# Another order for the last recurrent steps of a hybrid trunk: u split ahead of the scan, later loads, low weight halves on GpSimd

## The reference, cut to what matters

```python
proj = x @ w_in;  u, gate = split(proj)                       # 2048 x 1024 each
u = conv_b + sum(u_pad[:, tap:tap + S] * conv_w[tap] for tap in range(4))
r = sigmoid(ub @ w_a + b_a);  i = sigmoid(ub @ w_i + b_i)     # four blocks of 256 features
log_a = -8 * r * softplus(-lam);  a = exp(log_a)
bterm = sqrt(-expm1(2 * log_a)) * (i * u)
h[s] = a[s] * h[s - 1] + bterm[s]                             # along the 2048 positions
y = h * silu(gate)
out = layer_norm(alpha * x + y @ w_out)                       # "second merge"
```

## Time and profile before

| | us |
|---|---|
| three runs of the kernel before | 2414.43, 2416.19, 2415.93 |
| their median | 2415.93 |
| span of the profiled execution, first to last instruction | 2414.6 |
| TensorE busy in it | 2365.7 (98%) |
| VectorE, ScalarE, GpSimd busy | 1354.1, 1121.3, 617.7 |

### The profile page before, as it was taken

One profiled execution on the slowest core, in us unless ns is written; L12 is line 12 of the kernel. 1 busy time (PEld: TensorE's weight loads), 2 busy tenths in 40 slices (PEclk: granted clock), 3 DMA queues, 4 the chain that ended last, 5 costly groups with the idle time before them and its releaser, 6 DMA issues. The chain is left out here.

```text
span 2414.6 us, 36438 instructions
## 1 busy us (share of the span) xinstructions
PE 2365.7 (98%) x13373; PEld 2031.6 (84%) x13373; DVE 1354.1 (56%) x2772; ACT 1121.3 (46%) x2060; POOL 617.7 (26%) x718
## 2 busy tenths in 40 slices
PE   9999999999999999999999999999999999999998
PEld 7888889998888888888888888878888888887787
DVE  4221211331106888888888888836535565767733
ACT  2111111311116888888888888812014565657300
POOL 0000000000001555545555545516420000000343
PEclk9999999999999999999999999999999999999999
DMA  6443443332234455555445665275533354538762
GB/s 211 139 121 112 116 128 108 118 124 83 84 110 103 110 117 125 136 137 117 112 112 124 137 136 117 78 246 183 187 106 119 119 159 131 148 124 256 243 232 78
DMA packets 221258, 328.77 MB, mean 136 GB/s; under 512 B 17421, under 2 KB 144717, under 8 KB 215261
## 3 DMA queue, kind: packets, MB, share of 16 engines
q1 hardware_dynamic: 220568, 325.91, 47.7%
q0 software_dynamic: 512, 0.53, 0.1%
HBM read 199.89 MB, written 126.48 MB: 135 GB/s over the span
## 5 line engine op out<-in xcount | busy, mean ns | idle before, releaser
L985 DVE TENSOR_TENSOR at_pl<-at_tps,at_ph 128x512 fp32r<-128x512 f32 (+3 forms) x640 | 371.0, 604 | 15.9 <-ACT at_ph L908 15.9
L908 ACT ACTIVATE at_ph<-at_tps 128x512 fp32r<-128x512 f32 (+3 forms) x640 | 318.6, 537 | 125.4 <-PE at_tps L822 117.4
L822 PE MATMUL at_tps<-ident,at_probs 128*128 128x128 f32 x2176 | 340.4, 274 | 8.4 <-DVE at_pl L985 7.1
L380 ACT ACTIVATE pa_stg<-pa_ps 128x512 fp32r<-128x512 f32 (+1 forms) x120 | 71.7, 598 | 575.4 <-PE pa_ps L272 569.5
L842 PE MATMUL at_ops<-at_ph,at_val 128*128 128x256 f32 (+1 forms) x1152 | 315.4, 296 | 0.2 <-DVE at_pl L985 0.2
L898 ACT ACTIVATE at_probs<-at_probs,at_least 128x128 f32<-128x128 f32 (+15 forms) x256 | 308.1, 1204 | 0.0
L272 PE MATMUL pa_ps<-pa_xh,pa_wh 128*128 128x512 f32 x760 | 298.9, 393 | 0.0
L272 PE MATMUL pa_ps<-pa_xh,pa_wl 128*128 128x512 f32 x760 | 297.3, 391 | 0.0
L272 PE MATMUL pa_ps<-pa_xl,pa_wh 128*128 128x512 f32 x760 | 296.9, 391 | 0.0
L842 PE MATMUL at_ops<-at_pl,at_val 128*128 128x256 f32 (+1 forms) x1152 | 295.0, 282 | 0.0
L808 PE MATMUL at_sps<-at_k,at_q 128*128 128x512 f32 (+3 forms) x640 | 277.7, 434 | 9.7 <-DVE at_probs L977 7.2
(11 more groups left out here) (203 smaller groups left out, 4516.0 us busy)
## 6 DMA issues: line engine op xcount, KB each, us to landing
at_q<-q_halves SPq DMA_DIRECT2D x45, 512.0 KB
at_k<-k_halves SPq DMA_DIRECT2D x45, 512.0 KB
q_halves<-pa_stg SPq DMA_DIRECT2D x32, 512.0 KB, 3.8
k_halves<-pa_stg SPq DMA_DIRECT2D x32, 512.0 KB, 3.7
v_halves<-pa_stg SPq DMA_DIRECT2D x32, 512.0 KB, 3.0
y_gated<-re_work SPq DMA_DIRECT2D x32, 512.0 KB, 2.9
at_val<-v_halves SPq DMA_DIRECT2D x15, 1024.0 KB, 17.4
pa_wst<-in_attn_w_in SPq DMA_DIRECT2D x14, 1024.0 KB, 7.2
```

What stands on the lines that cost most here:

```text
L380: nc.scalar.activation(out, source(kind, s), func, scale=scale).then_inc(evac_h, 1)
L822: mm = nc.tensor.transpose(tps[c % TB][:, k, :], probs[s % ROWS][:, t0:t0 + P], ident[:, :])
L908: nc.scalar.activation(ph[g % 2][:, j * PB:j * PB + n, i % 2 * P:(i % 2 + 1) * P], tps[c % TB][:, 0:n, :], ACT.Copy).then_inc(high_out, 1)
L985: nc.vector.tensor_tensor(pl[g % 2][at], tps[c % TB][:, 0:n, :], raw(ph[g % 2][at]), ALU.subtract)\
```

## The change

VectorE's program: in step 13 `split_u(14)` moves ahead of `scan(12)`, and the steps 14 and 15 are written out in a new order, with the additions of merge tiles 0 to 3 between the parts of the recurrence; `weights_low(1, c)` is gone from it. GpSimd now makes those eight low halves. ScalarE makes the high halves of blocks 0 to 3 at the end of step 13 and those of 4 to 7 inside `nonlinear(13)`. TensorE does merge tile 1 ahead of `gate_products(15)`. SyncE's order of the last four steps is written out anew: the weights go ahead of `store_y(n-1)`, `load_u(15)` too, `load_y(1, 0)` (now four DMAs: 6 of the 8 feature blocks, then the 2 of step 12) and `load_y(1, 1)` come behind both tile stores of step 14 and ahead of `store_y(13)`, the gain and shift come ahead of `store_y(14)`.

```diff
@@ SyncE, load_y(r, j), r == 1 @@
-                    sp.wait_ge(y_stored, 32 * (STEPS - NC + j // 2 + 1))
                     if j < 4:
                         sp.wait_ge(products, chunk_done(2 + j // 2))
                     else:
                         sp.wait_ge(m_products, ST + 2 * (j - 4) + 2)
+                    if j == 0:
+                        for l in range(2):
+                            sp.dma_start(raw(m_rows(1, 0)[:, l, 0:KC - CT, :]), m_y[1][:, l, 0:KC - CT, 0:YW])\
+                                .then_inc(y_loaded[0], 16)
+                        sp.wait_ge(y_stored, 32 * (STEPS - NC + 1))
+                        for l in range(2):
+                            sp.dma_start(raw(m_rows(1, 0)[:, l, KC - CT:KC, :]), m_y[1][:, l, KC - CT:KC, 0:YW])\
+                                .then_inc(y_loaded[0], 16)
+                        return
+                    sp.wait_ge(y_stored, 32 * (STEPS - NC + j // 2 + 1))
@@ SyncE, the steps @@
-            for n in range(STEPS):
+            for n in range(STEPS - 4):
...
+            for n in range(STEPS - 4, STEPS):
+                first, second = step_tiles(n)[0]
+                if n < STEPS - 2:
+                    load_u(n + 1)
+                store_tile(first)
+                if n < STEPS - 1:
+                    load_gate(n - 1)
+                store_tile(second)
+                if n == STEPS - 2:
+                    load_y(1, 0)
+                    load_y(1, 1)
+                if n == STEPS - 1:
+                    for m in range(RING):
+                        load_residual(1, m)
+                    load_gate(n - 1)
+                    load_y(1, 2)
+                    sp.wait_ge(gates, STEPS)
+                    load_gain(1)
+                if n == STEPS - 4 or n == STEPS - 3:
+                    load_weights(n - STEPS + 4)
+                if n == STEPS - 3:
+                    load_u(n + 2)
+                    sp.wait_ge(y_stored, 32 * (STEPS - NC))
+                store_y(n - 1)
             load_gate(STEPS - 1)
-            for j in range(2, 4):
-                load_y(1, j)
-            sp.wait_ge(gates, STEPS)
-            load_gain(1)
+            load_y(1, 3)
@@ GpSimd, behind the memsets of u @@
+            for c in range(KC):
+                pool.wait_ge(m_high, KC + c + 1)
+                nc.gpsimd.tensor_tensor(m_block(1, xl, c), m_block(1, xl_raw, c), raw(m_block(1, xh, c)), ALU.subtract)\
+                    .then_inc(m_split, 1)
@@ TensorE, step 15 (merge_tile's wait counts 3 more DMAs of chunk 0) @@
                 if n == STEPS - 1:
                     merge_tile(1, 0)
+                    merge_tile(1, 1)
                 gate_products(n)
@@ ScalarE, nonlinear(13); the loop over the steps; the end @@
-                    for c in range(CP * 2):
+                    for c in range(CP * 2, KC):
                         weights_high(1, c)
...
-                if n == STEPS - 2:
-                    for c in range(CP * 2, KC):
+                if n == STEPS - 3:
+                    for c in range(CP * 2):
                         weights_high(1, c)
-            deviation(1, 0)
+            for n in range(2):
+                deviation(1, n)
             nonlinear(STEPS - 1)
@@ VectorE @@
-            for n in range(STEPS):
-                if n == STEPS - 1:
-                    for c in range(CP * 2, KC):
-                        weights_low(1, c)
+            for n in range(STEPS - 2):
                 split_u(n)
...
+                convolve(n + 1)
+                if n == STEPS - 3:
+                    split_u(n + 1)
                 if n:
                     scan(n - 1)
...
+            feed(STEPS - 3)
+            remainder(STEPS - 3)
+            convolve(STEPS - 1)
+            split_u(STEPS - 1)
+            scan(STEPS - 3)
             add_rows(1, 0)
-            norm_rows(1, 0)
+            feed(STEPS - 2)
+            add_rows(1, 1)
+            remainder(STEPS - 2)
+            scan(STEPS - 2)
+            for n in range(2):
+                norm_rows(1, n)
+            add_rows(1, 2)
             feed(STEPS - 1)
             remainder(STEPS - 1)
-            add_rows(1, 1)
+            add_rows(1, 3)
             scan(STEPS - 1)
-            norm_rows(1, 1)
-            for n in range(2, ST - 1):
+            norm_rows(1, 2)
+            norm_rows(1, 3)
+            for n in range(4, ST - 1):
```

More of the change, by code:

```diff
@@ L1434, in _ @@
             load_strip(3)
-            for n in range(STEPS):
+            for n in range(STEPS - 4):
                 before, behind = step_tiles(n)
-                tiles = (*before, *behind)
                 new_block = (n + 1) % NC == 0
-                if n + 1 < STEPS and not new_block:
+                if not new_block:
                     load_u(n + 1)
-                if n == STEPS - 2:
-                    load_y(1, 0)
-                for k, t in enumerate(tiles):
+                for k, t in enumerate((*before, *behind)):
                     store_tile(t)
                     if k == 0:
-                        if n + 1 < STEPS and new_block:
+                        if new_block:
                             load_u(n + 1)
@@ L1449, in _ @@
                             load_gate(n - 1)
-                        if n + 4 < STRIPS and not new_block:
+                        if not new_block:
                             load_strip(n + 4)
-                        if n + 4 < STRIPS and new_block:
+                        else:
                             if n + 5 < STRIPS:
@@ L1456, in _ @@
                                 load_strip(n + 4)
-                    if n and k == min(2, len(tiles) - 1):
-                        if n == STEPS - 2:
-                            load_y(1, 1)
-                        if n == STEPS - 1:
-                            for m in range(RING):
-                                load_residual(1, m)
+                    if n and k == 2:
                         store_y(n - 1)
-                        if n == STEPS - 4 or n == STEPS - 3:
-                            load_weights(n - STEPS + 4)
-                if n + 4 < STRIPS and new_block:
+                if new_block:
                     if n + 5 < STRIPS:
@@ L1525, in merge_tile @@
                 j = n // 2
-                pe.wait_ge(y_loaded[j % 4], 16 * (j // 4 + (1 if r or j % 4 >= 2 else 0) + (r * (1 if j % 4 < 2 else 2))))
+                pe.wait_ge(y_loaded[j % 4], 16 * (j // 4 + (1 if r or j % 4 >= 2 else 0) + (r * (1 if j % 4 < 2 else 2))
+                                                  + (3 if r and j % 4 == 0 else 0)))
                 if r == 0:
@@ L1624, in _ @@
                     project_tile(t)
-            for n in range(1, ST):
+            for n in range(2, ST):
                 merge_tile(1, n)
@@ L1942, in _ @@
                         split_gate_weights(BLOCKS - 1)
-                    if n == STEPS - 2:
-                        for c in range(CP * 2):
-                            weights_low(1, c)
                     remainder(n - 1)
-                if n + 1 < STEPS:
-                    convolve(n + 1)
+                convolve(n + 1)
+                if n == STEPS - 3:
+                    split_u(n + 1)
                 if n:
```

## The result

| | median, us | ratio to the kernel before, 95% |
|---|---|---|
| before | 2414.43 (5 runs beside the changed kernel) | 1 |
| changed | 2426.28 (5 runs) | 1.0047 [1.0036, 1.0058] |

The forecast was 2427, the range 2414 to 2433.

What follows compares the result with a forecast made beforehand. TensorE bounds the second merge; waits and low clock offered some 14 us. Shift of merge tile 0's start +16.4, waits -5.9, clock -1.9 and +2.7 give +11.3: span 2425.9, median 2427, range 2414 to 2433.

Steps and rivals of the forecast that it cites:

- Steps 1 and 2: Recurrence step 12: weights ahead of y(11) cost 0 (bounds -2.8, +1); `split_u(14)` ahead of `scan(12)` delays the gate product 1.55 us.
- Step 3: VectorE, `scan(12)`: GpSimd's low halves make scans, copy and gate product wait; the product ends at 2204.2, 8.8 us late.
- Step 4: ScalarE's chain of recurrence step 13: sigmoids until 2207.9, tile 61 evacuated at 2224.9 instead of 2218.1, +6.8 us.
- Step 5: SyncE: chunk 0 of y, issued behind tile 61, lands 9.1 us later; M (start of merge tile 0) moves +16.4 us.
- Step 6: TensorE from merge tile 0: nothing waits, -5.9 us of waits, -1.9 of clock, +2.7 of clock behind the long wait.
- Step 7: SyncE: gain and shift behind `gates(15)` land some 5 us later, as early against the rows as before; cost 0.
- GpSimd cheap: Rival on VectorE: GpSimd's work costs it little, tile 61 out at 2219.0; +5.4, 2421.3 us; chance 0.15.
- No change: Rival: loads come out well too and VectorE isn't held up, tile 61 out at 2214.2; +0.1, 2416 us; chance 0.12.
- faster: Rival: chunk 0's landing doesn't end the wait, tile 61 out by about 2205, all 14 us go; 2402 us; chance 0.08.
- much slower one: Rival: a second wait, `gate_products(15)` or merge tile 4 late behind VectorE; 2433 us and more; chance 0.10.

Runs made afterwards that it cites:

- a_both: Changed kernel with chunk 0 of y loaded ahead of step 14's tile stores and the low weight halves back on VectorE: 2410.50 us, 0.9980 to before.
- b_split: Kernel before with only `split_u(14)` moved ahead of `scan(12)`: 2414.89 us, 1.0002 to before.
- b_merge: Kernel before with only the changed order of merge tiles and additions: 2408.41 us, 0.9971 to before.
- b_late_y: Kernel before with only chunks 0 and 1 of y loaded behind the tile stores of step 14: 2421.77 us, 1.0028 to before.
- y_first: a_both with `store_y(11)` ahead of the weights and `load_u(14)` behind them: 2408.30 us, 0.9977 to the kernel before.
- a_low_dve: Changed kernel with the eight low weight halves back on VectorE, loads as changed: 2420.01 us, 1.0022 to before.
- a_early_y: Changed kernel with only chunk 0 of y loaded again ahead of the two tile stores of step 14: 2414.51 us, 0.9997 to before.
- b_low_pool: Kernel before with only the low weight halves moved to GpSimd, high halves where they were: 2414.67 us, 0.9995 to before.
- y_u_first: a_both with `store_y(11)` and `load_u(14)` both ahead of the weights: 2407.16 us, 0.9965 to the kernel before.

## Why the prediction was right, point by point

Times of the changed kernel's profile are given with the 1.4 us of its late start taken off.

- Steps 1 and 2, the weights ahead of y(11) and `split_u(14)` ahead of `scan(12)`. The times of the chain were right: the exp of step 12 started at 2180.1 (2179.9 said), the scan at 2192.2 (2192.0 said), and without GpSimd and the late load the wait ahead of `gate_products(14)` is 2.0 us longer than before (6.4 in a_both, 4.36 in the earlier trace rows; 1.55 said). The shares were wrong: I put 0 on the weights and 1.55 on the split. The split costs 1.1 (b_split against b_merge and b_late_y). Half a microsecond of the 1.55 was already the weights': I let the convolution end at 2190.1, and before it ended at 2189.6. From y_first to a_both they cost 1.8 us, from the profiled execution of before 1.0, and the bound was +1; the two differ by what u(14)'s landing differs, so which is nearer stays open. That the split is half of a double wait, so that moving it alone gains nothing, is what b_split shows.
- Step 3, GpSimd shuts VectorE out. The mechanism is right, the size was too large: the gate product ended at 2201.2 and not 2204.2. The scans waited out one GpSimd instruction (2.1 us) and the copy one (1.95), the gate product none. By the rows above it started at 2201.34, GpSimd's next instruction at 2201.36, and that one took 3.39 us and not 2.4, so this time it was GpSimd that waited (read from these times, not tested). 4.1 us, not 3 x 2.4. For the two halves of y I had one wait and there were two (2.0 each), one of them ahead of the cast, which has a single input, as the copy has. The Trainium skill's rule ("SBUF — State Buffer", "Who interferes with whom"), which no row of before showed for scans, holds for them here: 4.46 us against 2.34 in a_low_dve, where GpSimd's work is away.
- Step 4, ScalarE's chain. Sigmoids done at 2205.0 (2207.9 said), y(12) landed 2210.6 (2212.3), tile 61 out at 2223.1 (2224.9): the error of step 3, shrunk on its way.
- Step 5, chunk 0 behind tile 61. Right, and the dearest, as said: the wait is put down to this DMA, and a_early_y gives the whole loss back. Issue 2223.6 (2225.4), landing 10.1 us later and not 9.1. M = 2233.7 against 2234.6. The term was 1.0 us too small. The split in four DMAs, which I had called free, is not shown to be why: they took 3.0 us to issue, but in b_late_y, with the load in the same place and one DMA issued in 0.37 us, the chunk landed after 10.3, in a_low_dve with four after 9.9, and chunks 4 to 7 of the kernel before after 9.1 to 10.5. Chunk 1 is issued right behind in the changed kernel, in b_late_y and in a_low_dve; whether that matters was not tested.
- Step 6, nothing else waits. Right: no wait behind M. But the two terms behind M were off. M to the last matmul takes 179.9 to 180.0 us in the six kernels without a long wait at M and without any behind it. The changed kernel's 181.6 puts 1.6 us on the clock behind the long wait, not 2.7 (97 matmuls in 23.7 us, 22.0 in a_early_y; in the wait itself the granted clock was 0.66). Before, it was 188.5: of the 8.5 us 5.9 are waits, so the low clock behind them cost 2.6, not 1.9. Together 6.9 us were gained behind M, where I had summed 5.1. One slip of names: I gave the three waits of the earlier trace rows to merge tiles 1, 2 and 3; they are those of merge tiles 2, 3 and 4, the ones that wait for `add_rows`. The sum used their lengths and is not touched.
- Step 7: the rows of the merge wait for nothing, right.

So step 3 was too large (3.0 us, of which 1.8 was left when tile 61 was out), the landing of chunk 0 too small by 1.0, and the gain behind M too small by 1.8. With these the sum is 8.7 and not 11.3, and this execution gives +8.6 from E on. The timed runs give +11.3, but they part by more than the difference (2423.5 to 2428.2 changed, 2410.0 to 2416.2 before), and the profiled execution of before is on the slow side. So the hit to the tenth is luck, and the 2 or 3 us between are not resolved.

The rivals: GpSimd cheap (2421.3) fell, its 6 us are in a_low_dve. No change and faster both needed tile 61 out early, and it came 5 us later than before. The much slower one didn't come: VectorE's additions were in time though GpSimd lengthened step 15's work.

The parts alone on the kernel before give +6.8 (b_late_y), -1.2 (b_low_pool), +0.5 (b_split) and -7 (b_merge), in sum about -1 us; together they gave +11.3. Three things can be read for the difference. GpSimd's work meets the scan of step 12 only when the high halves 0 to 3 are made earlier, as in the change: 6 us in a_low_dve, nothing in b_low_pool. The late load and the order of the merge take away the same waits: b_late_y alone gains 4.9 us behind M, so these don't add. And the weights ahead of y(11), 1 to 2 us, are in none of the four. How the 12 us divide between the three was not measured.

## What to carry to other kernels

A load that is issued behind a wait for another engine takes over that engine's whole lateness plus its own time on the way: put it in the queue's program where its own data allows, not where it reads well. Before work is moved to GpSimd, look at what VectorE does at that moment: beside waits it was free, but beside the scan of step 12 one of the two scans, the copy, the cast and the subtraction each waited about 2 us, and TensorE waited for that chain. When two waits end within 0.1 us of each other, moving one of them alone gains nothing.

## What the runs showed of the hardware that I had not expected

- A VectorE copy of 128x2 elements took 2.12 us beside GpSimd and 0.17 without: the wait does not depend on how little the instruction moves. Nor does every instruction wait: the gate product behind it took its 1.21 us.
- The time that SyncE takes to issue a load is not a constant: 2 MB in one DMA took 0.37 us in b_late_y (chunk 0) and 4.50 in the kernel before (chunk 3, at 2248.84), in four DMAs 3.0 in the changed kernel. The landing, 10.3 and 10.1 us for chunk 0 in b_late_y and the changed kernel, did not follow it.
- The profiled executions of these kernels stand up to 4.35 us apart at the end of tile 61 (2193.86 in b_merge, 2198.21 in y_u_first). The distance is there already at 2063 us (2061.93 and 2066.29), where both have run the same code. A stage is better compared from a mark inside the execution than by its span.
